# Changing VectorE's order in a hybrid decoder's first mixer, the place of the second layer's tables, the last mixer's attention rows and the final scaling

## The reference

```python
h = rms_norm(x, norm1_g) @ w_in                  # one combined input projection
y = concat(gdn_mixer(...),                       # gated delta rule, 4 heads, chunks of 64
           s5_mixer(...),                        # diagonal complex state space, 16 groups x 64 states
           diff_attn_mixer(...))                 # 4 heads, softmax 1 - lam * softmax 2, causal
x = x + y @ w_out
# peer_ffn on rms_norm(x, norm2_g):
q = (xt @ wq).reshape(bn, 128, 8, 2, 64)
s = einsum('bthpd,hpnd->bthpn', q, keys)         # 8 heads, 2 x 128 sub-keys
sv, si = top_k(s, 16)                            # 16 x 16 candidates, of which again the top 16
act = gelu(einsum('bthkd,btd->bthk', u_tab[expert], xt))
y = einsum('bthk,bthkd->btd', gate * act, v_tab[expert])
```

## Time and profile before

| what | us |
|---|---|
| median of 3 runs | 1579.19 (1578.61 to 1581.76) |
| profiled execution | 1580.82 |
| its span | 1579.0 |
| VectorE busy | 1104.1 |
| GpSimd busy | 993.9 |
| TensorE busy | 970.5 |
| ScalarE busy | 299.6 |

### The profile page before, as it was taken

One profiled execution on the slowest core, in us unless ns is written; L12 is line 12 of the kernel. 1 busy time (PEld: TensorE's weight loads), 2 busy tenths in 40 slices (PEclk: granted clock), 3 DMA queues, 4 the chain that ended last, 5 costly groups with the idle time before them and its releaser, 6 DMA issues.

```text
span 1579.0 us, 17672 instructions
## 1 busy us (share of the span) xinstructions
PE 970.5 (61%) x5842; PEld 546.2 (35%) x5842; DVE 1104.1 (70%) x2869; ACT 299.6 (19%) x837; POOL 993.9 (63%) x1034
## 2 busy tenths in 40 slices
PE   9996567967443279886644347978864333333335
PEld 8885445534300046552420025755340000000001
DVE  6849799884648978786486766888466757575440
ACT  7434221321100042241100032324110010000000
POOL 0006666776566776667567775656767777777773
PEclk9997889977756589998876678989875666666558
DMA  9558999999999999999999999999999999999997
GB/s 368 188 200 302 411 393 419 419 419 420 418 420 419 381 417 420 419 419 414 420 419 420 420 419 419 408 418 348 418 419 420 419 419 419 419 419 419 420 419 307
DMA packets 172467, 626.51 MB, mean 397 GB/s; under 512 B 19284, under 2 KB 19412, under 8 KB 172376
## 3 DMA queue, kind: packets, MB, share of 16 engines
q0 software_dynamic: 147456, 536.94, 84.0%
q1 hardware_dynamic: 24920, 88.45, 14.2%
HBM read 624.26 MB, written 1.05 MB: 396 GB/s over the span
## 4 chain that ended last, share of the span: by engine, by line
DMA 28%; DVE 21%; POOL 21%; PE 16%; issue 9%; DVEq 4%; ACT 1%; POOLq 0%; ACTq 0%
DMA uring<-in_u_tab,small 24%; PE ps L609 16%; DVE uring L1834 10%; POOL uring L2688 7%; POOL vring L2688 7%; POOL gd L2688 2%; DMA vring<-in_v_tab,small 2%; POOL wring L2688 1%; DMA uring<-in_v_tab,small 1%; DMA sa<-in_u_tab,small 1%; POOL sa L2688 1%; DVE small L1749 1%; DVE small L1760 0%; DVE sel L1794 0%; DVE small L1802 0%
## 5 line engine op out<-in xcount | busy, mean ns | idle before, releaser
L1834 DVE CUSTOM_DVE_ANT_0 uring<-uring,ps 128x1024 f32<-128x1024 f32 x462 | 558.2, 1217 | 282.9 <-DMA uring<-in_u_tab,small 262.1
L2688 POOL DMA_INDIRECT uring<-in_u_tab,small x462 | 452.6, 980 | 371.9 <-DVE small L1834 168.4
L609 PE MATMUL ps<-vring,wmat 128*32 128x512 f32 x1748 | 320.1, 853 | 361.9 <-DMA vring<-in_v_tab,small 305.9
L2688 POOL DMA_INDIRECT vring<-in_v_tab,small x437 | 417.6, 956 | 154.6 <-issue 127.5
L609 PEld LDWEIGHTS ps<-vring,wmat 128*32 128x32 f32 x1748 | 58.1, 137 | 551.2 <-DMA vring<-in_v_tab,small 369.5
L609 PE MATMUL ps<-hnT,wring 128*128 128x128 f32 x1184 | 150.5, 285 | 0.7 <-DMA wring<-in_w_blocks 0.7
L609 PEld LDWEIGHTS ps<-hnT,wring 128*128 128x128 f32 x1184 | 141.4, 198 | 25.8 <-issue 21.6
L609 PE MATMUL ps<-wring,hnT 128*128 128x512 f32 (+1 forms) x208 | 88.6, 573 | 15.4 <-DMA wring<-in_w_blocks 11.6
L2678 ACT ACTIVATE small<-small 128x32 f32<-128x32 f32 x16 | 3.7, 230 | 465.7 <-DVEq L1843 465.7
L609 PE MATMUL ps<-gd 128*128 128x128 f32 (+1 forms) x518 | 74.2, 296 | 12.8 <-ACT gd L2138 11.2
L2138 ACT ACTIVATE gd<-ps 128x512 f32<-128x512 f32 (+3 forms) x86 | 48.0, 564 | 176.2 <-PE ps L609 161.9
(11 more groups left out here) (450 smaller groups left out, 1507.3 us busy)
## 6 DMA issues: line engine op xcount, KB each, us to landing
wring<-in_w_blocks SPq DMA_DIRECT2D x120, 512.0 KB, 7.2
vring<-in_w_blocks SPq DMA_DIRECT2D x32, 512.0 KB, 8.6
uring<-in_u_tab,small POOLq DMA_INDIRECT x462, 12.5
vring<-in_v_tab,small POOLq DMA_INDIRECT x437, 11.3
wring<-in_cols SPq DMA_DIRECT2D x3, 512.0 KB, 6.8
h<-in_x SPq DMA_DIRECT2D x2, 512.0 KB, 9.2
keysT<-in_keys SPq DMA_DIRECT2D x2, 512.0 KB, 13.7
rows<-in_rows SPq DMA_DIRECT2D x2, 486.0 KB, 10.6
```

The source lines that it names most:

```text
L609: return nc.tensor.matmul(o, a, b, start=start, stop=True, skip_group_check=True)
L1834: V.tensor_tensor_reduce(row_, row_, xp, 1.0, 0.0, ALU.mult, ALU.add, dots[:, j:j + 1]).then_inc(dot_done.sem, 1)
L2688: nc.gpsimd.indirect_dma_start(dst, None, table, bass.IndirectOffsetOnAxis(ap=index, axis=0)).then_inc(done.sem, 16)
```

## The change

Four places are edited.

1. In the first mixer, VectorE does one of the table doublings behind the two `silu` calls instead of ahead of the first, and the third state-space part's last piece (L1919 to L1924) behind the two attention maxima instead of ahead.
2. The second layer's tables run in rows 92 to 107 of block 0 (`next_tables`, half a row per unit of the generator's own schedule) instead of rows 2 to 29 of block 1, on VectorE and on ScalarE (rows 91.5 and 92.5). Their scratch is in `gd`. `outputs` stays where it was, in block 1. SyncE issues the parameters of layer 1, now without keys, behind the first half of mixer 1's `out3` and behind `mix_ready(1, 1)`; the keys alone stay where the parameters stood. Waits on parameters ask for 48 instead of 64, and TensorE's `head_scores` waits for the keys.
3. In mixer 3, VectorE's attention pieces go to later rows: maxima 71 to 73, scales 73 to 75, difference 74 to 76, second maxima 75 to 78, scales 76 to 79, difference 78 to 81, the norm's reciprocal 82 to 84, the last scaling 84 to 86. In mixer 1 the first maxima go from row 70 to 71 and the scales from 72 to 73. ScalarE's and TensorE's rows are as before.
4. At the end, VectorE multiplies the first half of the columns by the gain while ScalarE sums squares; after the reciprocal and a drain, ScalarE scales that half while VectorE scales the second in one operation. SyncE sends the second half first.

```diff
@@ SyncE
+                if i == 1 and (name, half) == ("out3", 0):
+                    sp.wait_ge(*mix_ready(i, 1))
+                    params(1)
...
             if i == TB:
                 sp.wait_ge(*sc_done(1, 2))
-                params(1)
+                sp.dma_start(keysT[:, :, :].rearrange("p h n -> p (h n)"), keys_d[1, :, :]).then_inc(keys_in.sem, 16)
@@ TensorE, head_scores
+            if i >= TB:
+                pe.wait_ge(keys_in.sem, 32)
@@ VectorE, tables
-            if layer > 0:
-                yield 37
-                outputs(layer)
+        def next_tables(i):
+            yield TABLES
+            for k in tables(i):
+                yield TABLES + 0.5 * k
@@ VectorE, mix
-            if t == 0:
-                yield place(i, 2)
-                made = tables(i)
-                for k in made:
-                    if k > 32:
-                        break
-                    yield place(i, k)
...
-            yield attend(i, 71 if wide else 69.8 + 2 * later)
+            yield attend(i, 73 if wide else 70.9 + later)
             att_max_of(i, rs[0], *round_heads(i, rs[0]))
-            yield attend(i, 72.4 if wide else 71.4 + later)
+            yield attend(i, 75 if wide else 72.1 + later / 2)
             att_scales(i, rs[0], *round_heads(i, rs[0]))
...
-            yield attend(i, 74 if wide else 72.8 + later)
+            yield attend(i, 76 if wide else 72.8 + later)
             att_diff(i, rs[0], *round_heads(i, rs[0]))
             if wide:
-                yield attend(i, 74.6)
+                yield attend(i, 77.6)
                 att_max_of(i, rs[1], *round_heads(i, rs[1]))
             if t == 1:
-                yield attend(i, 76 if wide else 73.8)
+                yield attend(i, 79 if wide else 73.8)
                 att_scales(i, rs[1], *round_heads(i, rs[1]))
-                yield attend(i, 77.4 if wide else 75.2)
+                yield attend(i, 81 if wide else 75.2)
                 att_diff(i, rs[1], *round_heads(i, rs[1]))
-            yield attend(i, 82 if wide else 80)
+            yield attend(i, 84 if wide else 80)
...
-            yield attend(i, 83.5 if wide else 81.9)
+            yield attend(i, 85.5 if wide else 81.9)
@@ VectorE, final_second
+            fence()
+            V.tensor_tensor(scaled[:, 0:512], h[:, 1, 0:512], g2[:, 0:512], ALU.mult)
...
             V.reciprocal(rstd, rstd)
-            fence()
-            for half in range(2):
-                at = slice(512 * half, 512 * half + 512)
-                V.scalar_tensor_tensor(scaled[:, at], h[:, 1, at], rstd, g2[:, at], ALU.mult, ALU.mult
-                                       ).then_inc(final_ready.sem, 1)
+            V.drain().then_inc(final_root.sem, 1)
+            V.scalar_tensor_tensor(scaled[:, 512:1024], h[:, 1, 512:1024], rstd, g2[:, 512:1024], ALU.mult, ALU.mult
+                                   ).then_inc(final_ready.sem, 1)
@@ VectorE, first_mixer
-            step()
             dve.wait_ge(lev_in.sem, 16)
             V.tensor_copy(heads4(B[1]), bc(negT[:, None, :], [P, HEADS, P]))
             silu(0, 0, 4, B[6])
             step()
             silu(0, 4, 6, B[7])
+            step()
...
-            for j in (1, 2):
-                for _ in ssm_of(j):
-                    pass
+            for _ in ssm_of(1):
+                pass
+            third = ssm_of(2)
+            next(third)
+            next(third)
             dve.wait_ge(att_done.sem, 1)
...
+            for _ in third:
+                pass
             for _ in ssm_of(3):
                 pass
@@ ScalarE
+        def next_tables(i):
+            yield TABLES - 0.5
+            tables_exp(i)
+            yield TABLES + 0.5
+            tables_sin(i)
...
             S.activation(rstd, ss, ACT.Sqrt, bias=bias0).then_inc(final_ss.sem, 1)
+            scaled = hnT[:, :, :].rearrange("p k t -> p (k t)")
+            act.wait_ge(final_root.sem, 1)
+            copy(scaled[:, 0:512], scaled[:, 0:512], rstd).then_inc(final_scaled.sem, 1)
```

More of the change, by code:

```diff
@@ L149, in attend @@
     return place(i, slot) + (5.5 if i == 1 else 0.0)
+TABLES = 92.0
 SCANS = (33.0, 41.5, 50.0, 58.0)
@@ L323, in _build @@
     cst_in, fin_in, out_done = signal("cst_in"), signal("fin_in"), signal("out_done")
-    params_in = signal("params_in", 64, 0)
+    params_in = signal("params_in", 48, 0)
     g2_in = signal("g2_in", 16)
@@ L443, in _build @@
     final_ready = signal("final_ready")
+    final_root = signal("final_root")
+    final_scaled = signal("final_scaled")
     first_half_summed = signal("first_half_summed")
+    tables_at = [(sa[:, 1536:2048], sa[:, 2048:2560]), (gd[:, 2048:2560], gd[:, 2560:3072])]
     def flat3(a):
@@ L536, in params @@
             sp.dma_start(rows[:, :], rows_d[layer, :, 0:HELD_ROWS]).then_inc(params_in.sem, 16)
-            sp.dma_start(keysT[:, :, :].rearrange("p h n -> p (h n)"), keys_d[layer, :, :]).then_inc(params_in.sem, 16)
         def flat(tile):
@@ L598, in _ @@
         sp.dma_start(out[0, 0:P, :], hn[:, :]).then_inc(out_done.sem, 16)
-        for half in range(2):
-            sp.wait_ge(final_ready.sem, 2 + half)
+        for half, landed, value in ((1, final_ready, 2), (0, final_scaled, 1)):
+            sp.wait_ge(landed.sem, value)
             sp.dma_start(out[0, P:2 * P, 512 * half:512 * half + 512],
@@ L1006, in mix @@
             if layer > 0:
-                pe.wait_ge(*params_in(layer, 64))
+                pe.wait_ge(*params_in(layer, 48))
             for k in range(KT):
@@ L1359, in tables @@
             if layer > 0:
-                dve.wait_ge(*params_in(layer, 64))
+                dve.wait_ge(*params_in(layer, 48))
                 lam_sums()
@@ L1433, in tables @@
                 nc_, ns_ = pw[1] if n in (1, 4, 16, 64) else pw[0]
-                A = sa[:, 1536:2048].rearrange("p (m t) -> p m t", m=MT)[:, :, 0:n]
-                B = sa[:, 2048:2560].rearrange("p (m t) -> p m t", m=MT)[:, :, 0:n]
+                A = tables_at[layer][0].rearrange("p (m t) -> p m t", m=MT)[:, :, 0:n]
+                B = tables_at[layer][1].rearrange("p (m t) -> p m t", m=MT)[:, :, 0:n]
                 pcb, psb = bc(pc[:, :, None], [P, MT, n]), bc(psn[:, :, None], [P, MT, n])
@@ L1558, in mix @@
                 yield place(i, 37)
-                next(made, None)
+                outputs(layer)
             yield place(i, 42)
@@ L2110, in _ @@
                 b = n // 4
-                stages = Stages(mix(b + 1), attention(b + 1), *([scans(1)] if b == 0 else [])) if b + 1 < NI else Stages(final_first())
+                stages = Stages(mix(b + 1), attention(b + 1), *([scans(1), next_tables(TB)] if b == 0 else [])) if b + 1 < NI else Stages(final_first())
             choose = top(n + 1) if n % 4 != 3 else iter(())
@@ L2155, in tables_exp @@
         def tables_exp(i):
-            act.wait_ge(*params_in(i // 2, 64))
+            act.wait_ge(*params_in(i // 2, 48))
             S.activation(stp, col("lst"), ACT.Exp).then_inc(step_ready.sem, 1)
@@ L2208, in mix @@
             rs = rounds(i)
[L2209 to L2213, removed]
             yield place(i, 33.5)
@@ L2225, in mix @@
             if layer > 0:
-                act.wait_ge(*params_in(layer, 64))
+                act.wait_ge(*params_in(layer, 48))
             for b, o in enumerate((M0, M1)):
```

## The result

The changed kernel takes 1584.3 us in the median of 8 runs (1581.44 to 1587.87), the kernel before 1581.41 (8 runs). The two medians differ by 2.9 us; the ratio as estimated from all the runs is 1.0026 with an interval of 1.0015 to 1.0036, about +4 us (2.4 to 5.7). Forecast was -2.1. The profiled execution of the changed kernel is one of its fastest (span 1579.6), so its trace shows the places of the loss better than their size.

What follows compares the result with a forecast made beforehand. The DMA, full at about 419 GB/s in most slices, was taken as the bound. Terms -1.7 - 3.7 - 0.5 + 4 + 0 - 0.2 = -2.1 us gave 1577.2 us at the median, range 1572.8 to 1582.2.

Steps and rivals of the forecast that it cites:

- What bounds the kernel: Whole kernel: DMA full at about 419 GB/s in most slices; edits gain only in thinner stretches or lose by making new ones.
- First mixer, -1.7: Start to 132 us: TensorE's waits of 1.48 and 2.42 us shrink, order-bound slack limits the gain; -1.7 us (-3.0 to -0.8).
- Tables, where they leave, -3.7 and -0.5 behind: Block 1's first 32 rows: without tables the 500 to 560 dent fills, -3.7 us; thin slice from 711 gains 0.5.
- Tables, where they arrive, +4: Block 0 from row 92: VectorE stands waiting for parameters until about 372.5, DMA backlog hides most; +4 us (0 to +9).
- The Trainium skill: Parameter loads at row 92: DMA engines alternate between queues, so loads could land up to 2.5 us earlier; not counted.
- Last mixer's maxima, 0 (-2.7 to +2): 1060 to 1100: later maxima remove VectorE's waits, gaining up to 2.7 us, but later values lose up to 2; 0 taken.
- the values lose up to 2: Last mixer: values of rows 77, 81, 85 come about 3 us later, costing up to 2 us.
- The last scaling, -0.2: End of kernel: ScalarE scales one half beside VectorE, replacing 0.7 us of the second scaling; -0.2 us (-0.4 to 0).
- The slower side: Rows 92 to 115: VectorE becomes the bound, 6.4 us more, 1583.6, chance .12; slower than 1582.3 in all .14.
- the cover holds: Rival at row 92: gathers in flight and weights hide GpSimd's 15 us idle, cost 0 to 1, 1574.2; chance .25.
- the maxima pay too: Rival in the last mixer: VectorE's 5.0 us of waits vanish, values not later, 2.7 us kept, 1574.5; chance .10.
- the first mixer's gain did arrive: Answers a rival: indices wait for an untouched chain, the start stays at 132, the 1.7 us is lost, 1578.9; chance .08.

Runs made afterwards that it cites:

- g2_t112: The changed kernel with the attention rows of before and the tables from row 112 instead of 92; 1576.73 us, 0.9981 of the kernel before.
- e2_tables: The kernel before with the tables' move alone, parameters and keys included; 1582.5 us, 1.0018 of the kernel before.
- e4_nomax: The changed kernel with the attention rows put back as before; 1580.72 us, 1.0008 of the kernel before.

## Why the prediction was wrong, step by step

- **What bounds the kernel** (right). Full stretches stayed at 419 in every undisturbed kernel (1100 to 1560), and the parts add up by what they do to the thin ones.
- **First mixer, -1.7** (right in mechanism, a little low in size). Measured -2.4 (0.9976 to 0.9994). The waits of 1.48 and 2.42 went, and the new one of 1.21 is the order-bound slack that the step named. The first row's dot is at 129.5 to 130.4 in the five profiled executions that have the edit and at 131.8 to 133.6 in the five other undisturbed ones; forecast was 130.3.
- **Tables, where they leave, -3.7 and -0.5 behind** (wrong in size, and the second term in sign). This is a term that failed: it took the whole dent at 500 to 560 as gain. That stretch does fill up, but 690 to 760 then loses more, 2.4 in place of 1.0 in the means. As I read it, the engines' own pace in the second mixer isn't changed, so the gathers that are served earlier aren't there later and the queue runs dry earlier; g2_t112, with a dent ahead and 0.1 there, agrees, but no run was made to show it. Together the removal gives 1.4. I had credited the stretch behind with a gain, arguing from a larger backlog.
- **Tables, where they arrive, +4** (right). The stop was 17.3, 19.3 and 19.0 us in three kernels, forecast 18.5; the loss at 390 to 430 was 3.2, 5.9 and 4.8, 4.6 in the mean. In the changed kernel the weights ahead were issued some 5 us earlier than before, so the parameters landed at 367.3 and not at 372.5, and dot 92 came 4 us earlier as well; the two moved together. GpSimd stood 9.7 us, not 15.5. In e2_tables and e4_nomax, whose parameters landed at 373.0 and 372.3, it stood 16.2 and 11.4. That the landing was met there is partly luck: the 2.2 us between landings left out that the loads are issued 0.85 apart in all (in before they landed 2.9 and 2.5 apart). Net the tables cost 4.6 - 1.4 = 3.2 by the windows, 2.8 by the time; the step's sum was -0.2.
- **The Trainium skill** on "DMA: Bandwidth & Descriptors", "Queues, rings and completion order": the three parameter loads landed 1.9 and 2.5 us apart (362.9, 364.8, 367.3) with the gathers queued. This agrees with loads that take turns with the gathers, but no run tests it. The rows that I gave for the rule were of 416 and of 359 us; at 416 itself a gather took 24.6 us to land, so the reading holds. The changed kernel's earlier landing comes from their earlier issue, so the gain that I had named beside the rule isn't shown.
- **Last mixer's maxima, 0 (-2.7 to +2)** (wrong; the step that failed most). The measured +3.6 to +3.8 is outside its bounds. The term "the values lose up to 2" was mis-sized: GpSimd's waits for TensorE's values grew by 7.3 us, while its waits for VectorE fell by 5.5. Two things lay behind it. "The first maximum lands at the same time" compared absolute times: by the scores that it needs, it starts 0.0 us behind TensorE in before (scores end at 1057.46, maximum at 1057.50) and 2.1 behind in after (1054.64, 1056.77). And the step saw VectorE's waits as the cost, where they were the sign that TensorE and ScalarE set the pace; on ScalarE, whose order wasn't edited, the late first exponentials hold up a copy of the delta rule's (TensorE waits 4.46 us for it instead of 2.37), and the products that GpSimd's gathers wait for stand behind it. The late second exponentials hold up TensorE's transposes (1.51 us where there was no wait), with the products behind them. VectorE's waits went only in part: 2.11 of the 5.0 us stand ahead of the second maxima. The prediction asked who waits for the maxima, but not what is queued behind those who wait.
- **The last scaling, -0.2** (nothing to be seen; it was not run alone). From the second addition to the end it takes 6.03 to 6.11 us with the edit in four profiled executions and 5.97 to 6.04 without in six. The last output transfer is issued 0.2 us earlier (3.35 us behind the second addition instead of 3.55), the first 0.07 later, and the end follows neither gain.
- **Rivals and chances.** The slower side had .14, its mechanism (VectorE as bound to row 115) isn't what was seen: 430 to 470 stayed full. That its 1583.6 is near the measured time is luck. The rival "the cover holds" wanted a loss of 0 to 1 us at 390 to 430, and 3.2 to 5.9 came; "the maxima pay too" was against the sign; and the first mixer's gain did arrive. The range, 1572.8 to 1582.2 from a median of 1579.19, left out the measured 1584.3; even at the ratio, 1579.19 x 1.0026 = 1583.3, it would have. It was narrow because each part's bounds came from one execution, and one stretch of the same program varies by 1.5 to 4.5 us.
- One sentence of the section on the kernel is too wide: `place` stretches the slots for mixer 1 alone; for mixers 2 and 3 the slot is the row, as the prediction uses it.

## What to carry to other kernels

An engine that waits often in a busy stretch may be the one that follows; before its work is moved to fill the waits, look at what stands behind every engine that waits for it, in that engine's fixed order. A wait for data that is put into the middle of an engine's order costs by its length less the backlog behind it: 17 to 19 us of stop stood beside a loss of 3 to 6, and six rows later the same work lost under 2 in one execution. A dent in the DMA's rate is worth its depth only if the queue behind can use it; sum the thin stretches over the whole run, in several executions, before counting it.

## What I had not expected of the hardware

A condition in which the same program takes 8% longer: 1710 instead of 1580 us, with runs from 1690 to 1743, at 370 to 384 GB/s where 419 was moved before, in three calls in succession, two of them on a chip that had given 1580 before. And the spread of one stretch between undisturbed executions, 200 to 340, from 1.5 to 4.5 us lost, with the same instructions up to its end.
